# Two outer products of the sample recurrence on another engine: a decoder step on one Trainium2 core

## What is computed

```python
def step(S, inp):
    r_t, w_t, k_t, v_t, kk_t, a_t = inp
    sa = jnp.einsum('bhvk,bhk->bhv', S, -kk_t)
    S = S * w_t[:, :, None, :] + sa[..., None] * (kk_t * a_t)[:, :, None, :] + v_t[..., None] * k_t[:, :, None, :]
    return S, jnp.einsum('bhvk,bhk->bhv', S, r_t)
```

## Time and profile before

| | us |
|---|---|
| median of 3 runs | 2600.22 (2599.62 to 2607.33) |
| the profiled execution | 2608.56 |
| its span, first to last instruction | 2606.4 |
| TensorE busy over the span | 2256.9 (87%) |
| VectorE busy | 1510.0 (58%) |
| ScalarE busy | 1127.3 (43%) |
| GpSimd busy | 74.3 (3%) |

### The profile page before, as it was taken

One profiled execution on the slowest core, in us unless ns is written; L12 is line 12 of the kernel. 1 busy time (PEld: TensorE's weight loads), 2 busy tenths in 40 slices (PEclk: granted clock), 3 DMA queues, 4 the chain that ended last, 5 costly groups with the idle time before them and its releaser, 6 DMA issues. The chain is left out here.

```text
span 2606.4 us, 29399 instructions
## 1 busy us (share of the span) xinstructions
PE 2256.9 (87%) x11350; PEld 1777.7 (68%) x11351; DVE 1510.0 (58%) x2083; ACT 1127.3 (43%) x1704; POOL 74.3 (3%) x110
## 2 busy tenths in 40 slices
PE   6974897847998869989888898766999999999998
PEld 4753787836998645557776454455888888888886
DVE  4034898843443037751365323215889889889885
ACT  3112232203332137751343333204777777777774
POOL 4000000000000000000100000000000000000000
PEclk8986898868999879988576999877999999999999
DMA  5101000024442473410301344166999999999992
GB/s 185 65 1 44 2 1 1 1 103 162 162 162 112 179 250 148 179 29 15 129 1 45 141 162 162 27 169 204 337 362 360 357 363 358 357 364 360 358 355 101
DMA packets 291217, 447.95 MB, mean 172 GB/s; under 512 B 41880, under 2 KB 254088, under 8 KB 288626
## 3 DMA queue, kind: packets, MB, share of 16 engines
q1 hardware_dynamic: 287324, 374.61, 42.7%
q0 software_dynamic: 3456, 71.30, 6.7%
q10 hardware_dynamic: 294, 0.11, 0.0%
HBM read 438.53 MB, written 14.85 MB: 174 GB/s over the span
## 5 line engine op out<-in xcount | busy, mean ns | idle before, releaser
L2744 DVE TENSOR_TENSOR moe.w_gate_up_lo<-mw.raw,moe.w_gate_up_hi 128x2048 fp32r<-128x2048 f32 x176 | 403.0, 2290 | 88.9 <-ACT moe.w_gate_up_hi L2687 88.1
L2687 ACT CAST moe.w_gate_up_hi<-mw.raw 128x2048 fp32r<-128x2048 f32 x176 | 337.8, 1920 | 116.9 <-PE moe.b L1121 112.5
L1119 PE MATMUL moe.b<-moe.w_gate_up_hi,moe.x_block_hi 128*128 128x512 f32 x704 | 284.9, 405 | 1.4 <-DVE moe.x_block_lo L2744 1.4
L1121 PE MATMUL moe.b<-moe.w_gate_up_hi,moe.x_block_lo 128*128 128x512 f32 x704 | 276.8, 393 | 0.0
L1120 PE MATMUL moe.b<-moe.w_gate_up_lo,moe.x_block_hi 128*128 128x512 f32 x704 | 276.4, 393 | 0.0
L2744 DVE TENSOR_TENSOR moe.w_down_lo<-mw.raw,moe.w_down_hi 128x2048 fp32r<-128x2048 f32 x88 | 201.4, 2289 | 14.1 <-ACT moe.w_down_hi L2693 13.8
L2693 ACT CAST moe.w_down_hi<-mw.raw 128x2048 fp32r<-128x2048 f32 x88 | 168.4, 1914 | 46.7 <-PE moe.b L1121 45.5
L1534 DVE COPY cmp.rows_t<-cmp.b 64x256 f32<-64x256 f32 (+1 forms) x288 | 114.0, 396 | 73.0 <-PE cmp.b L1501 69.5
L1119 PEld LDWEIGHTS moe.b<-moe.w_gate_up_hi,moe.x_block_hi 128*128 128x128 f32 x704 | 133.5, 190 | 29.6 <-DVE moe.x_block_lo L2744 1.8
L1121 PEld LDWEIGHTS moe.b<-moe.w_gate_up_hi,moe.x_block_lo 128*128 128x128 f32 x704 | 133.4, 189 | 28.5
L1120 PEld LDWEIGHTS moe.b<-moe.w_gate_up_lo,moe.x_block_hi 128*128 128x128 f32 x704 | 133.6, 190 | 27.9
(11 more groups left out here) (571 smaller groups left out, 4266.5 us busy)
## 6 DMA issues: line engine op xcount, KB each, us to landing
mw.raw<-in_moe_w_gate SPq DMA_DIRECT2D x176, 512.0 KB, 6.1
mw.raw<-in_moe_w_up SPq DMA_DIRECT2D x176, 512.0 KB, 7.8
mw.raw<-in_moe_w_down SPq DMA_DIRECT2D x176, 512.0 KB, 6.8
rin.w_rkv<-in_rw_w_rkv SPq DMA_DIRECT2D x3, 4096.0 KB, 18.3
ffn.w<-in_ffn_w_gate SPq DMA_DIRECT2D x11, 1024.0 KB, 5.2
ffn.w<-in_ffn_w_up SPq DMA_DIRECT2D x11, 1024.0 KB, 7.5
ffn.w<-in_ffn_w_down SPq DMA_DIRECT2D x10, 1024.0 KB, 6.2
out_win_kv_sample<-in_state_win_kv SPq DMA_DIRECT2D x1, 8128.0 KB
```

The lines of the kernel that those rows point to most:

```text
L1119: nc.tensor.matmul(out, w_hi, x_hi, start=start, stop=False)
L1121: return nc.tensor.matmul(out, w_lo, x_hi, start=False, stop=stop)
L2687: nc.scalar.copy(wgu_hi[:, h % 3], raw_gu(t, x)).then_inc(gu_high, 1)
L2744: return nc.vector.tensor_tensor(out, x, high, ALU.subtract)
```

## The change

The steps k3 and k5 of every quarter are taken from VectorE and made on ScalarE. VectorE did each as one instruction on 128 x 1024 with both factors broadcast. ScalarE does each as 16 instructions (`nc.scalar.activation` with the function Copy), one per value v: the row of 64 keys is scaled by one number per partition and written to a row of 64 of `tmp[x]`. Only the last of the 16 increments the new semaphore `outer_done`. `sample_count` counts how many steps of either engine lie at or before step n, and `after_sample` waits on the semaphore of the engine that made step n. On ScalarE k3 waits for k1 of its quarter (n - 4) and k5 for k4 (n - 2). On VectorE k4 waits for k3 (ScalarE) and for k2 (n - 4), and k6 for k5 (ScalarE). The place on ScalarE is behind the four copies of the level that holds the step.

```diff
+ON_SCALAR = (3, 5)
+
+def sample_op(n):
+    pair, k, x = n // 18, n % 18 // 2, n % 2
+    return pair // 2, 2 * (pair % 2) + x, x, k
+
+def sample_count(n, on_scalar):
+    return sum((sample_op(i)[3] in ON_SCALAR) == on_scalar for i in range(n + 1))
...
+        def after_sample(eng, n):
+            on_scalar = sample_op(n)[3] in ON_SCALAR
+            eng.wait_ge(outer_done if on_scalar else sampled, sample_count(n, on_scalar))
...
                 def sample(n):
...
+                    if k in ON_SCALAR:
+                        return
...
                     if n >= 2:
-                        dve.wait_ge(sampled, n - 1)
+                        after_sample(dve, n - 2)
+                    if k == 4 and n >= 4:
+                        after_sample(dve, n - 4)
...
-                    elif k == 3:
-                        last = op(o, over_v(sav[:, x, :]), over_k(5, t), ALU.mult)
...
-                    elif k == 5:
-                        last = op(o, over_v(W.sv[:, 3, t, vs]), over_k(2, t), ALU.mult)
...
+                def sample_outer(n):
+                    t, quarter, x, k = sample_op(n)
+                    if k not in ON_SCALAR:
+                        return
+                    after_sample(act, n - 4 if k == 3 else n - 2)
+                    for v in range(SQ):
+                        by = sav[:, x, v:v + 1] if k == 3 else W.sv[:, 3, t, SQ * quarter + v:SQ * quarter + v + 1]
+                        last = nc.scalar.activation(tmp[:, x, v, :], W.sv[:, 5 if k == 3 else 2, t, :], ACT.Copy, scale=by)
+                    last.then_inc(outer_done, 1)
...
                             copy_inverse_t(m, l, st)
+                        for n in range(PER_LEVEL):
+                            sample_outer(PER_LEVEL * (5 * m + l - 1) + n)
...
+                for n in range(20 * PER_LEVEL, SAMPLE_OPS):
+                    sample_outer(n)
...
-                sp.wait_ge(sampled, SAMPLE_OPS)
+                after_sample(sp, SAMPLE_OPS - 1)
+                after_sample(sp, SAMPLE_OPS - 2)
```

More of the change, by code:

```diff
@@ L605, in stage_wkv @@
             "first_level", "u_products", "u_masked", "inv_products", "inv_copied", "inv_t_products", "inv_t_copied"))
-        dchain, sampled, s_ready = s.sem("dve_step"), s.sem("sample_ops"), s.sem("state_ready")
+        dchain, sampled, outer_done, s_ready = s.sem("dve_step"), s.sem("sample_ops"), s.sem("sample_outer"), s.sem("state_ready")
         st_mm, st_ev, st_in, st_out = s.sem("state_turned"), s.sem("state_copied"), s.sem("state_in"), s.sem("state_out")
@@ L825, in _ @@
                 over_k = lambda i, t: W.sv[:, i, t, :].unsqueeze(1).to_broadcast([P, SQ, HD])
-                over_v = lambda ap: ap.unsqueeze(2).to_broadcast([P, SQ, HD])
                 op = nc.vector.tensor_tensor
                 def sample(n):
-                    pair, k, x = n // 18, n % 18 // 2, n % 2
-                    t, vs = pair // 2, slice(SQ * (2 * (pair % 2) + x), SQ * (2 * (pair % 2) + x) + SQ)
+                    t, quarter, x, k = sample_op(n)
+                    if k in ON_SCALAR:
+                        return
+                    vs = slice(SQ * quarter, SQ * quarter + SQ)
                     S, o = Ss[:, vs, :], tmp[:, x]
```

## The result

The changed kernel takes 2672.3 us (median of four runs, 2669.99 to 2676.94), the kernel before 2599.92 beside it (four runs, 2595.43 to 2607.33). The ratio is 1.0278 (95% interval 1.0250 to 1.0306): 72 us slower, where +63 was predicted. The profiled execution took 2676.94 us, its span is 2674.8.

The account below looks back on a forecast made before the run. VectorE was taken to set the pace of the time-mixing stage. Steps saved (-36.3), waits for ScalarE (+94.4) and TensorE restarts (+5) summed to +63 us, hence 2663 us; own range 2640 to 2690, wider range 2634 to 2706.

Parts of the forecast that it names:

- The 36.3 us off VectorE: Sample steps of the time-mixing stage: 32 leave VectorE at 1.135 us each, saving 36.3 us.
- The price of a product: One outer product on ScalarE: 16 rows of 128x64 at 0.239 us each, 3.8 us in all.
- The bounds 2.4 and 5.3: ScalarE outer product: 2.4 us if the per-partition operand costs nothing, 5.3 us if rows do not overlap.
- The waits for ScalarE: VectorE's k4 and k6 waiting for ScalarE's products over eight pairs of quarters: 94 us.
- The first waits of the eight pairs: VectorE's first wait per pair, where k3 is queued behind a level's copies on ScalarE: together 33 us.
- The other waits: The three later VectorE waits in each pair, mostly 2.66 us each before corrections: together 61.4 us.
- the last term, +5 us for TensorE: Six mask waits for TensorE between levels: one more slowly restarting group each, 0.85 us more, 5 us.
- Rows that don't overlap: Rival for ScalarE's rows: no overlap, 5.3 us a product, +104 us, 2704 us; chance 0.07.
- a free operand: Rival for ScalarE's rows: the scale operand costs nothing, 2.4 us a product, +25 us, 2625 us; chance 0.08.
- The lower level for the whole stage: Rival: VectorE's waits leave TensorE idle and at its lower clock level throughout, +40 on the forecast, 2703 us; chance 0.03.
- The rival on the other side: Rival: ScalarE's idle time hides the products, deciding from 1.5 us a product; by columns alone 2591 us; chance 0.04.
- the prediction's table to look for: Expected profile signs: 3.8 us per 16 ScalarE rows, some 94 us of VectorE waits, stage some 295 us instead of 232.

Follow-up runs that it names:

- e4: Changed kernel with each of the 16 rows per product scaled by the constant 0.5 instead of a number per partition; 2630.92 us, ratio 1.0097.
- e12: Changed kernel plus unread TensorE transposes, 60 at each of the first two block ends and 90 at the last; 2662.71 us, ratio 1.0252.
- e3: Changed kernel making only the first 8 of the 16 rows of each product; 2624.45 us, ratio 1.0081.
- e7: Kernel before with only ten k5 products on ScalarE, made one pair ahead into buffers of their own; 2597.26 us, ratio 0.9984.
- e9: As e7, but each level gives VectorE seven steps it still has, and products stand where ScalarE was idle; 2590.33 us, ratio 0.9957.
- e6: Changed kernel plus unread TensorE transposes, 16 behind each of blocks 0 to 2 and 24 behind block 3; 2680.32 us, ratio 1.0305.
- e10: Changed kernel plus unread TensorE transposes, 60 at each of the first three block ends and 90 at the last; 2668.55 us, ratio 1.0252.
- e2: Only k5 moved to ScalarE, k3 on VectorE as in the kernel before; 2656.62 us, ratio 1.0189.
- e1: Only k3 moved to ScalarE, k5 on VectorE as in the kernel before; 2634.30 us, ratio 1.0128.
- e8: Changed kernel with ScalarE's two copies of g at the last block's end moved ahead of the last two products; 2673.76 us, ratio 1.0264.

## Why the prediction was right, and what it mis-sized

**The 36.3 us off VectorE** are there: 36.8 us less busy time.

**The price of a product** was the argument's main choice, and it held: 0.239 us a row predicted from the earlier trace rows and 0.239 measured, 335 ns a row (0.33 predicted), 3.82 us a product (3.8), 124 us in all (121). The bounds 2.4 and 5.3 were drawn from the right rows: e4, the case without the operand, is the 2.4 (2.34 measured), and the 5.3 would have needed rows that don't overlap.

**The rule that speaks against the change** (The Trainium skill, "ScalarE: Activation LUTs", section "Rules for kernel authors") gave the right advice here. The prediction gives its reason too broadly: the Trainium skill says there that VectorE is faster per element in bf16, for operations with one source. The products here are f32 with two inputs, so these rows don't test that reason; by columns ScalarE is the cheaper engine in them, and it is 16 starts per product that cost 3.8 us against 1.135.

**The waits for ScalarE**, laid out pair by pair, were 94.4 us and measured 97.8. The first waits of the eight pairs were to be 5.3, 1.5, 8.9, 1.9, 7.7, 0, 6.6 and 1.1; the rows show 5.6 (8.27 less 2.66), 2.1, 9.2, 1.0, 8.0, 0, 6.9 and 1.7. The other waits were 61.4 and measured 63.3. The first pair, worked in full, was to have its second k6 8.7 us later; counted from the first mask it is 9.2 us later.

**The step that was mis-sized is the last term, +5 us for TensorE.** It counted the six mask waits of before and gave each one slow group more of 0.85 us. Measured, the masks and the tail have 13.2 us more. Of the 14.2 us that the sum was short this is 8.2; the waits for ScalarE are 3.4, and 2.6 are the short waits. The step reasoned from the length of single groups between levels, where the clock did come back as it said (1.00 from 310 to 320 us, for example). It did not look at what ScalarE's products push back at the ends of blocks: the copies of g, for which TensorE idled 7.1, 6.9 and 10.9 us, and behind which it ran at the lower level for 8 us at a block end and for the whole tail of 27 us. The earlier trace rows had shown the lower level in the tail of the kernel before, at 0.56, but the prediction spoke of the tail only as cover for SP's second wait, and 5.2 us stand there. e12 is the test: the copies of g late as ever, TensorE kept busy until they come, and 11.7 us of it gone.

**The rivals.** Rows that don't overlap (2704) and a free operand (2625) fall by the rows; e4 is what the second would have been. The lower level for the whole stage (2703) was wrong in its extent and half right in its mechanism: the clock was 0.81 over the stage and did fall behind idle times, but the falls that e12 shows to cost time came behind waits for ScalarE's copies, not for VectorE. The rival on the other side was put at 1.5 us a product as the point where it turns. With a slope of 27 and the measured 77.2 it is 3.82 - 77.2 / 27 = 1.0 us; e3 at 1.91 us still lost 27 us in the stage, so no run reached the point, and for products handed over in this order it is only extrapolated.

**What the prediction's table to look for said**: the stage was to be 295 us from the first mask to the last step; it is 303.2 (270.08 to 573.3). The granted clock was to be about 0.8; it is 0.81.

**What was luck.** The time came closer to the forecast than the stage did. The sum, +63, was 14.2 us short of the stage's 77.2, but the two profiled executions differ by 68.4 us only: code that was not changed took 2.4 us less ahead of the stage and 6.4 us less behind it.

## What to carry to other kernels

In this kernel, work moved from a full engine to an idle one gained only where nobody waited for it there: ten of the 32 products, made a pair ahead into buffers of their own, took 6 us off the stage where all 32 behind a wait had added 77, though ScalarE paid three times the price for each. What leaves the full engine must also leave its cover in place (e7 against e9: fill the gap with later steps, or the chain that was hidden by it becomes the wait). And before costing a moved piece by its own length, list what is queued behind it on its new engine at the ends of loops; there the price was another engine's clock.

## What the hardware showed

In e6, 1.9 us of transposes in some 7 us of idle time left the granted clock behind it at 0.51 and 0.52, and 2.8 us in 11 left it at 0.50. In e10, 6.7 us of them in 7 and 10.0 in 11 gave 1.00. Nothing between the two was tried. In e12, 90 useless transposes and 60 more at each of two places were worth 11.7 us to the stage; the 60 that e10 had at a place without idle time cost 6.4.

The tail took 38.6 us in six kernels (after and e2 to e6), the same to 0.1 us, though the wait of TensorE ahead of it was anywhere from 5.6 to 10.9 us. In all six its first group ran at the lower level (1.97 to 1.98 us). In the kernel before, e10 and e12, where that group took 1.09 us, the tail was 33.4 to 33.7. The level is not all that counts: in e1 the group took 1.98 us as well, but the copies of g came 4.5 us earlier against VectorE's last step, and the tail was 35.0; in e7 and e8 it took 1.09 us, TensorE then stood 4.2 and 6.4 us for VectorE's sum, and the tail was 35.0 too.

An operand per partition cost ScalarE 0.09 us in each row of 64 columns, also in a string of rows and also as the scale of a Copy (e4: 0.146 us a row without it, 0.239 with it).
